# Page loads behind the next scores, a different share of fetched dots, and the last gates chunk from its staging buffer

## The reference

```python
# latent attention of the samples: past pages and the own 4 rows
ckv_all = concat([cache_ckv[page_table].reshape(8, 2048, 128), ckv])
kpe_all = concat([cache_kpe[page_table].reshape(8, 2048, 32), kpe])
s = einsum('bqhc,bkc->bhqk', q_lat, ckv_all) + einsum('bqhr,bkr->bhqk', q_rope, kpe_all)
o_lat = einsum('bhqk,bkc->bqhc', softmax(mask(s * SM_SCALE)), ckv_all)
...
# experts, per token: two sets of 128 keys, the best 16 x 16 sums, the best 16 of these
s = einsum('nhpc,hpkc->nhpk', q, sub_keys); sv, si = top_k(s, 16)
cv, ci = top_k(sv[:, :, 0, :, None] + sv[:, :, 1, None, :], 16)
g = softmax(cv); act = gelu(einsum('nhkd,nd->nhk', expert_u[experts], x))
y = einsum('nhk,nhkd->nd', g * act, expert_v[experts])
```

## Time and profile before

| | |
|---|---|
| median of 3 runs | 2139.24 us (2136.78 to 2145.38) |
| profiled execution | 2147.01 us, span 2145.1 us |
| mean granted TensorE clock | 0.904 |
| TensorE busy | 1915.8 us (89%) |
| VectorE, ScalarE, GpSimd busy | 67%, 28%, 27% |
| HBM read, written | 443.73 MB, 33.94 MB |

### The profile page before, as it was taken

The page is one execution under the profiler, slowest core; times in us unless marked ns, Lnnn a source line. Parts: engine busy times, 40 slices in busy tenths (PEclk is TensorE's granted clock), DMA queues, the critical chain, the costliest instruction groups (busy, mean ns, idle before and its releaser), DMA issues.

```text
span 2145.1 us, 26500 instructions
## 1 busy us (share of the span) xinstructions
PE 1915.8 (89%) x9117; PEld 1500.0 (70%) x9117; DVE 1436.1 (67%) x3189; ACT 609.1 (28%) x1020; POOL 586.6 (27%) x454
## 2 busy tenths in 40 slices
PE   6988899666688988999886999999999999999994
PEld 3556674554467745667675788888888888888883
DVE  4025366243346755999986778888888777777777
ACT  1132122210011111114455333333333333333331
POOL 0000002344423123310000114454454444444440
PEclk9989999666675679999998999999999999999997
DMA  6611334354534456554438878999998888888872
GB/s 250 228 40 40 123 118 162 108 164 146 186 137 147 148 171 229 202 178 149 164 141 302 295 278 321 356 349 340 364 340 301 317 289 291 320 287 292 318 255 92
DMA packets 152645, 479.29 MB, mean 223 GB/s; under 512 B 14624, under 2 KB 75856, under 8 KB 130928
## 3 DMA queue, kind: packets, MB, share of 16 engines
q1 hardware_dynamic: 94704, 270.60, 34.8%
q0 software_dynamic: 57856, 207.65, 27.2%
HBM read 443.73 MB, written 33.94 MB: 223 GB/s over the span
## 4 chain that ended last, share of the span: by engine, by line
PE 73%; DVE 16%; another core or an unknown queue 4%; DMA 3%; issue 2%; ACT 2%; POOL 0%; SPq 0%; DVEq 0%; ACTq 0%
PE ps L1034 24%; PE ps L1024 19%; PE ps L634 6%; PE ps L970 3%; PE ps L935 3%; PE ps L986 3%; DVE lo L1650 2%; PE ps L1011 2%; PE ps L721 2%; PE ps L720 2%; PE ps L803 2%; PE ps L743 1%; PE ps L638 1%; DMA lo<-x 1%
## 5 line engine op out<-in xcount | busy, mean ns | idle before, releaser
L1478 POOL DMA_INDIRECT lo<-ur,lo x192 | 244.3, 1272 | 797.8 <-DVE lo L2011 323.5
L1478 POOL DMA_INDIRECT lo<-vr,lo x192 | 278.1, 1448 | 650.1 <-DVE lo L2079 306.7
L1024 PE MATMUL ps<-xh,uh 128*128 128x352 f32 x832 | 270.6, 325 | 0.0
L1024 PE MATMUL ps<-xh,ul 128*128 128x352 f32 x832 | 270.5, 325 | 0.0
L1024 PE MATMUL ps<-xl,uh 128*128 128x352 f32 x832 | 268.8, 323 | 0.0
L1129 ACT ACTIVATE hi<-ps 128x512 f32<-128x512 f32 (+10 forms) x259 | 154.3, 645 | 373.7 <-PE ps L970 111.9
L1034 PE MATMUL ps<-vh,hh 128*128 128x512 f32 (+1 forms) x768 | 240.9, 395 | 19.9 <-DVE vl L2047 19.9
L1034 PE MATMUL ps<-vl,hh 128*128 128x512 f32 (+1 forms) x768 | 241.1, 395 | 0.0
L1034 PE MATMUL ps<-vh,hl 128*128 128x512 f32 (+1 forms) x768 | 240.0, 394 | 0.0
L2071 DVE SCALAR_TENSOR_TENSOR lo<-lo 128x1024 f32<-128x1024 f32 x174 | 221.8, 1282 | 18.5 <-DMA lo<-vr,lo 9.7
L2047 DVE TENSOR_TENSOR vl<-hi,vh 128x1024 fp32r<-128x1024 f32 x128 | 156.9, 1226 | 48.8 <-ACT vh L1129 48.3
(11 more groups left out here) (385 smaller groups left out, 2928.5 us busy)
## 6 DMA issues: line engine op xcount, KB each, us to landing
hi<-ev SPq DMA_DIRECT2D x64, 1024.0 KB
hi<-wts SPq DMA_DIRECT2D x22, 2048.0 KB, 7.8
hi<-eu SPq DMA_DIRECT2D x38, 1024.0 KB, 10.0
lo<-eu SPq DMA_DIRECT2D x26, 1024.0 KB
gates<-hi SPq DMA_DIRECT2D x11, 2048.0 KB, 7.2
hi<-gates SPq DMA_DIRECT2D x32, 704.0 KB, 8.5
lo<-cache SPq DMA_DIRECT2D x48, 128.0 KB
hi<-cache SPq DMA_DIRECT2D x48, 128.0 KB
```

The costliest lines, as they stand in the source:

```text
L1024: last = nc.tensor.matmul(ps[:, 6 + p, 0:GW[1]], a[p][:, k * 128:(k + 1) * 128], b[:, k, :], start=(k == 0 and b is xh and a is uh), stop= ...
L1478: nc.gpsimd.indirect_dma_start(ring[n % RING], None, table, bass.IndirectOffsetOnAxis(idxs[:, i, k:k + 1], 0)).then_inc(r_in[n % RING], 16)
```

## The change

Three things. The loads of pages b+2 wait, on SyncE and on GpSimd, also for the scores of sequence b+1. GpSimd's loop has three fetches before the page loads instead of two, and VectorE six dots per sequence instead of five (`U_SAMPLE` 6); the keys stage has 16 instead of 24 (`U_KEYS`), four per quarter; the total stays 102. And ten of eleven chunks of the first two gate tables are loaded before the last chunk is stored; that chunk is copied by VectorE from the staging buffer. ScalarE's rounding of the first v moves ahead of the copies of the last chunk (q = 80), VectorE's low part of it ahead of the first gating, and ScalarE's wait for the last chunk's store behind its rounding of the first hidden.

```diff
-U_SAMPLE = 5
+U_SAMPLE = 6
...
-U_KEYS = 24
+U_KEYS = 16
...
                 sp.wait_ge(s["sm_o"], b - 1)
+                sp.wait_ge(s["sm_s"], b)
                 load_pages(b, rows)
...
+            def load_first_gates(quad):
+                sp.dma_start(gt[quad].rearrange("p c b t -> p c (b t)")[:, 0:NCH - 1, :],
+                             table[:, 0:NCH - 1, quad * 4:quad * 4 + 4, :].rearrange("e c b t -> e c (b t)")).then_inc(g_in[quad], 16)
...
+                if c == NCH - 1:
+                    sp.wait_ge(gs_in[0], 16 * (NCH // 2))
+                    sp.wait_ge(gs_in[1], 16 * (NCH // 2))
+                    for quad in range(2):
+                        load_first_gates(quad)
                 sp.wait_ge(s["ev_done"], CH // 4 * (c + 1))
                 sp.dma_start(gates[c * NK:(c + 1) * NK, :], stage[c % 2].rearrange("p e t -> p (e t)")).then_inc(gs_in[c % 2], 16)
             load_v(1, 1)
             sp.wait_ge(gs_in[0], 16 * ((NCH + 1) // 2))
-            sp.wait_ge(gs_in[1], 16 * (NCH // 2))
-            for q in range(2):
-                load_gates(q, q)
...
                     for q in range((T[i] - S0) // 4, (T[i] - S0 + r) // 4):
+                        if q == (NCH - 1) * CH // 4:
+                            round_v((0, 0), 16, None)
                         gates_copy(q)
...
+            round_hidden(0, 1, None)
             act.wait_ge(gs_in[0], 16 * ((NCH + 1) // 2))
-            round_v((0, 0), 16, None)
-            round_hidden(0, 1, None)
...
-                u_fetches(at, at + 2)
+                u_fetches(at, at + 3)
                 if b + 2 < SB:
                     pool.wait_ge(s["sm_o"], b + 1)
+                    pool.wait_ge(s["sm_s"], b + 2)
                     load_pages(b + 2)
-                u_fetches(at + 2, at + U_SAMPLE)
+                u_fetches(at + 3, at + U_SAMPLE)
...
             dve.wait_ge(s["gm_ps"], GW[1] // 4)
+            low_v((0, 0), 1)
+            fetched_gates(0)
+            dve.wait_ge(gs_in[1], 16 * (NCH // 2))
+            dve.wait_ge(s["ev_done"], GW[1] // 4)
+            for quad in range(2):
+                ins = v.tensor_copy(gt[quad][:, NCH - 1], stage[(NCH - 1) % 2][:, quad * 4:quad * 4 + 4, :])
+            step(ins)
             early_gated(0)
             low_hidden(0, 1)
-            low_v((0, 0), 1)
-            fetched_gates(0)
```

## The result

| | before | changed |
|---|---|---|
| median | 2138.37 us (4 runs) | 2116.80 us (4 runs) |
| range | 2136.78 to 2145.38 | 2107.49 to 2123.22 |
| profiled execution, span | 2147.01, 2145.1 | 2107.49, 2105.7 |
| mean granted clock | 0.904 | 0.913 |

The ratio is 0.9889, with a 95% interval from 0.9846 to 0.9933: 1.1% faster. Forecast were 2088 us and 2.4%. The time lies in the range, but the gain is 21.6 us where 50.8 were forecast.

A forecast was written before the change was run, and what follows sets the result against it. TensorE, 89% busy, was taken as the bound, with stalls ahead of the expert loop to remove. Samples -39.7, extra dot +1.2, keys -3.4 and gates -8.9 sum to -50.8: from 2139.2 to 2088 us, range 2060 to 2150.

The forecast's parts named there:

- The stall gone at its old place: Samples stage: sequence 1's row maxima are read at about 422.9 us, not 433.05, with no page-load burst running.
- the rival of the returned stall: Samples stage: the stall comes back within the softmax, between maxima and exponentials; 2144 to 2158 us, chance 0.33.
- I take each of five hops held 0.7 us: P = 24: Softmax hops beside the burst: 24 us from one read of maxima to the next, a gain of 39.7 us.
- 6 us of free running: TensorE's scores in the samples stage: 6.0 us, from the free period's 20.45 less 14.5.
- So the sixth is covered: Samples stage: VectorE's sixth dot (1.16 us) per sequence fits its 3.9 us of slack; without it 7 us in all.
- The gates: Turn to the expert loop: gate tables loaded before the last chunk's store gain 8.9 us, between 5.6 and 10.8.
- 1165.7: Turn: time in us for the last chunk's store, queued behind 1.3 MB of loads; 1163.5 if unhindered, else up to 1169.
- The keys: Expert keys' scores: eight VectorE dots fewer gain 3.4 us, from 0 to 7.0.
- The stretch behind the samples: Behind the last sequence: one more dot without cover, a loss of 1.2 us.
- a rival under which the stall would stand wherever it stood: Samples stage: transfers have nothing to do with the stall, so only the other parts count, -11.1 us, 2128; chance 0.10.
- The section on back-pressure: Samples stage: notes that stalled writes to one SBUF port block others' traffic, cited for semaphore updates stuck behind both queues' writes.

The follow-up runs named there:

- e13: Kernel before with only the shift of rows (six fetches and dots per sequence, three fetches before the pages, four dots per keys quarter), chip 12: 2126.89 us, ratio 0.9909.
- e14: The changed kernel once more, on chip 12, where the kernel before takes 2144.90 us: 2107.73 us, ratio 0.9824.
- e5: The kernel before, unchanged, run again on chip 13: 2080.32 us, ratio 1.0003 to its other runs there.
- e3: The changed kernel run again, on chip 6: 2079.22 us, ratio 1.0004 to the kernel before.
- e10: The changed kernel with all six fetches of a sequence ahead of its page loads, chip 3: 2075.74 us, ratio 0.9975 to the kernel before.
- e2: Kernel before plus the gates part alone, chip 6: 2071.04 us, ratio 0.9965.
- e12: Kernel before with SyncE's 12 pages of each sequence loaded twice into the same place, chip 13: 2105.98 us, ratio 1.0131.
- e6: Kernel before plus the new wait on SyncE's page loads alone, chip 13: 2079.83 us, ratio 1.0031.
- e7: Kernel before plus the new wait on GpSimd's page loads alone, chip 13: 2092.40 us, ratio 1.0073.
- e15: The changed kernel with all six fetches ahead of the page loads and without GpSimd's new wait, chip 6: 2076.57 us, ratio 0.9982 to the kernel before.
- e16: The changed kernel with all six fetches ahead of the page loads and without SyncE's new wait, chip 6: 2073.77 us, ratio 0.997 to the kernel before.
- e4: The changed kernel with the samples stage's 48 row fetches cut to 32 of 1024 elements, chip 6: 2077.75 us, ratio 0.9979 to the kernel before.
- e9: The changed kernel without its two new waits, chip 3: 2075.23 us, ratio 0.9966 to the kernel before.
- e11: The changed kernel without its two new waits and with all six fetches ahead of the page loads, chip 0: 2076.14 us, ratio 0.9975 to the kernel before.

## Why the prediction was wrong

**The stall gone at its old place: right.** Sequence 1's maxima are read at 425.07, where 422.9 plus the run's own offset of 2.2 were forecast, and there is no hold of 8 us in the softmax: the rival of the returned stall (0.33) fell, on both kinds of chip. Two things limit it. The last read is held for 2.1 us. And the waits are not all of the cause: on chip 12 the shift of rows alone, without them, gives about half of the whole gain (e13).

**"I take each of five hops held 0.7 us: P = 24": this step failed.** Measured are 27.25 and, in e14, 26.8, so the stage gave 20.2 to 23.2 us and not 39.7; six times the 3.25 us between 27.25 and 24 are the 19.5 that are missing. (23.2 is e14 against the first profile of the kernel before, since chip 12 has none of its own.) From the read at 425.07 to the next scores (439.54) it is 14.5, the very figure of an unhindered period: in that period the hops were not held at all. The next scores then took 11.9 us for 5.0 (439.54 to 451.45): 3.2 are three gaps between their matmuls, and 3.3 that the last 28 matmuls took 6.47 us, at half clock, and not the 3.2 that 28 of the 32 took in sequence 1 (3.66 us for 32). I had priced the softmax with care and taken the scores as 6 us of free running. What I put on the hops lay, in this period, on TensorE itself. Over all six periods it is 3.8 us each of slower matmuls and 2.7 of TensorE's idle time over e5 (22.9 and 15.9 in all, above). What makes the gaps stays open; both profiles of the changed kernel on chips with holds have them, and e3 has none in the same scores.

**"So the sixth is covered": this step failed on chips without holds.** e3 has periods of 22.0 on chip 6, where nothing is held, and e10 with the rows first 20.8: 1.2 are late rows, for which the dots reach into the next maxima. The step counted the dot's 1.16 us and not the row it waits for, which the change puts behind eight page loads: the text said "on GpSimd three fetches" are queued behind the wait and never priced them. Over the launch that is 7.3 us (150.0 against 142.7). As a wait it is no part of the 27.25: there VectorE waits for the scores before every read, as the lines above show for four of them, so the longer scores cover the late rows.

**The gates: right.** 8.0 in both pairs (222.7 to 214.7, 222.0 to 213.8) for 8.9 forecast, and by the mechanism that was forecast: the second expert's v waits for the last store. It sets the size: the store, behind the loads, landed 10.5 us after its issue (1124.39 to 1134.9, where ScalarE takes up its work on the second expert) and not the 9 that 1165.7 stood for. Measured alone (e2) the part gives 0.35%.

**The keys: right.** 4.1 on quiet chips (136.9 to 132.8), 4.9 in the first pair, for 3.4; the 3.44 of the earlier trace rows became 0.80, and a little came out of the quarters too.

**The stretch behind the samples: +1.2 in the sum, for one more dot.** It came out 8.6 us shorter. That is luck, not a part of the change that the prediction had: the first profile of the kernel before is in the slow group of that stretch (0.50) and the changed one in the fast (0.76), and in e5 the kernel before is in the fast group too, with the stretch 10.9 us shorter.

**A rule of the Trainium skill, read once more.** I gave 0.10 to the rule of the Trainium skill's page "SBUF — State Buffer", section "Who interferes with whom", that DMA never contends with a compute engine, as a rival under which the stall would stand wherever it stood. It did not stand: with the page loads moved, it went. On four chips the traces agree with the rule, on chip 13 at 349 and even 373 GB/s. In the first measurement engines stand still beside as many packets (1272 for 1275), and on chip 12 beside the same burst, so either it has an exception, or the path is another than SBUF's ports; that these holds come from transfers at all is argued and not shown. The Trainium skill's page "NOTIFIC — the notification-queue block", section "Overflow: three behaviours, one of which stalls the engine", says that trace records can hold back the engines that write them, in one of the three settings of a queue. That would fit holds of all engines at once; which setting holds here, no run shows, and every run on record comes with a span and a clock from the profiler, so none gives the time without it. The section on back-pressure that the prediction set behind its reading (the Trainium skill's page "DMA: Bandwidth & Descriptors") is on copies between the SBUFs of two cores; this kernel runs on one core, so it bears on these loads by likeness at most.

## What stays open

What makes chip 12 and the first one different. Shown is that the holds are not in the kernel alone (e5 against the earlier trace rows, with equal packets), that the ten-microsecond ones stand beside bursts of page loads (the last read, with fetches of rows only, is prompt there and 2.1 us late in the changed kernel), that more writes don't bring them up elsewhere (e12), and that they come back on chip 12 (e13). Not shown is which of the two queues makes them: e6, e7, e15 and e16 all fell on chips without them. Nor was e10 run on a chip with holds. I expected it 7 us below the change there, but VectorE waits for the scores in the changed kernel anyway; whether the gaps on TensorE, beside which the late rows are fetched, would go with the order is the open point, and small rows (e4) were not tried there either.

On chips without holds none of these is told apart from the gates part alone (e2, 0.9965, the lowest median): e9 has 0.9966 and e16 0.997. On a chip with holds only the change and e13 were measured, and the change is the better.

## What to carry to other kernels

A wait that ends with no releaser in the profile is first of all a property of the place where it was measured: run the unchanged kernel on another chip before a change is built around it, here 60 us that four of five numbered chips did not have. When work is moved behind a wait on an in-order queue, price what stands behind it on that queue: three row fetches, asked for behind eight page loads, took back 7 of the 12 us that keys and gates earn on a chip without holds. And gaps on TensorE can cost twice, in themselves (3.2 us in the scores of sequence 2) and in matmuls at half clock behind them (3.3). Last, shorter stages don't add up to a shorter kernel where the clock of another stretch moves: some 11 us gained in two stages were 3 to 6 in the time (e9, e10, e11, e15, e16).

## What the runs showed that I had not expected

- The same kernel takes 2079 us on four chips and 2138 to 2145 on others, most runs of a chip within 0.5% of its median, at a mean clock of 0.92 and 0.904.
- TensorE, VectorE and ScalarE can stand still together for 11 us (e13, from 452.3, where the last matmul ends, to 463.43) beside transfers that on another chip hold nobody. TensorE's next matmul there:

```profile
464.47 0.40 PE L791 MATMUL ps<-lo 128*32 128x128 f32 x1 [12.18 <-DVE lo L1874]
```

- TensorE stayed at 1.2 GHz while it was busy for 19.14 of 20 us, in ten of 18 profiles, in a stretch whose clock was about 0.75 in the others: two profiles can differ by 16 us in the part behind the samples (214.4 and 230.7, e5 and e9), with the same code there.
